# Attention in a hybrid encoder block on 8 cores: the meta keys' V products as two 64-row matmuls, added to opened banks

## The reference

```python
s_grid = einsum('bqhd,bkqjhd->bhqkj', q_r, k_r) * scale + bias       # 8 x 16 neighbours
s_meta = einsum('bqhd,bmhd->bhqm', q_r, km) * scale + mbias          # 16 meta keys
p = softmax(concatenate([s_meta, s_grid], axis=-1), axis=-1).astype(v.dtype)
out = einsum('bhqm,bmhd->bqhd', p_m, vm) + einsum('bhqkj,bkqjhd->bqhd', p_g, v_r)
```

## Time and profile before

| | |
|---|---|
| median of 3 runs | 1762.98 us (1759.71 to 1766.43) |
| the profiled execution | 1759.94 us |
| its span, slowest core (core 1) | 1758.4 us (cores 1739.4 to 1758.4) |
| mean granted TensorE clock, core 1 | 0.984 |
| busy: TensorE / VectorE / ScalarE | 1690.5 / 998.7 / 821.0 us |

### The profile page before, as it was taken

The page is one execution under the profiler, slowest core; times in us unless marked ns, Lnnn a source line. Parts: engine busy times, 40 slices in busy tenths (PEclk is TensorE's granted clock), DMA queues, the critical chain, the costliest instruction groups (busy, mean ns, idle before and its releaser), DMA issues.

```text
span 1758.4 us, 39342 instructions; the slowest of 8 cores (1739.4 to 1758.4 us)
## 1 busy us (share of the span) xinstructions
PE 1690.5 (96%) x13896; PEld 874.5 (50%) x13896; DVE 998.7 (57%) x1907; ACT 821.0 (47%) x1219; POOL 124.6 (7%) x202
## 2 busy tenths in 40 slices
PE   8898999999999999999999998999999999999998
PEld 3344544444455555655666654444444444444443
DVE  4344443442466675766777765555665566556654
ACT  4355656331256765677777762332333233323332
POOL 0012021111100000000000020000000000000000
PEclk9899999999999999999999999999999999999999
DMA  9689668673555566566533469634464345524421
GB/s 273 206 237 294 216 208 266 184 193 123 165 155 135 164 168 187 152 182 175 146 122 98 129 211 275 186 105 118 127 173 143 94 124 162 165 83 137 138 96 61
DMA packets 163814, 289.21 MB, mean 164 GB/s; under 512 B 70627, under 2 KB 92643, under 8 KB 155047
## 3 DMA queue, kind: packets, MB, share of 16 engines
q1 hardware_dynamic: 110167, 155.04, 30.6%
q0 software_dynamic: 37184, 95.66, 18.8%
q10 hardware_dynamic: 16272, 35.99, 6.6%
HBM read 194.90 MB, written 100.90 MB: 168 GB/s over the span
## 4 chain that ended last, share of the span: by engine, by line
PE 77%; DMA 6%; issue 5%; ACT 4%; DVE 4%; SPq 2%; ACTq 1%; POOL 0%; DVEq 0%; POOLq 0%
PE bankpair L433 19%; PE bankpair L949 9%; PE bankpair L407 9%; PE bankpair L380 9%; PE bankpair L593 7%; PE bankpair L625 7%; PE bankpair L926 6%; PE bankpair L1061 4%; PE bankpair L1030 3%; ACT sb_PT L1036 2%; DMA sb_Wp<-w_pool 2%; SPq L479 2%; DMA at_s<-sb_ATT 1%; PE bankpair L1049 1%; DVE sb_PT L1042 1%
## 5 line engine op out<-in xcount | busy, mean ns | idle before, releaser
L1036 ACT ACTIVATE sb_PT<-bankpair 128x1024 bf16<-128x1024 f32 (+1 forms) x368 | 318.9, 921 | 152.4 <-PE bankpair L1030 112.1
L433 PE MATMUL bankpair<-sb_Wo,sb_MIX 128*128 128x512 bf16 x1536 | 337.0, 381 | 3.0 <-DVE sb_MIX L417 3.0
L433 PEld LDWEIGHTS bankpair<-sb_Wo,sb_MIX 128*128 128x128 bf16 x1536 | 151.0, 98 | 187.1 <-issue 8.6
L1042 DVE TENSOR_TENSOR sb_PT<-sb_PT,sb_FT 128x1024 bf16<-128x1024 bf16 (+1 forms) x264 | 174.7, 667 | 107.5 <-ACT sb_PT L1036 104.8
L949 PE MATMUL bankpair<-sb_Wz,sb_HT 128*128 128x512 bf16 x768 | 195.2, 382 | 3.1 <-ACT sb_PM L979 2.7
L926 PE MATMUL bankpair<-sb_HT,sb_Wq 128*128 128x512 bf16 x768 | 196.1, 384 | 2.1 <-DVE sb_QT L217 2.0
L593 PE MATMUL bankpair<-sb_HT,sb_Wk 128*128 128x512 bf16 (+1 forms) x832 | 192.2, 386 | 4.8 <-DVE sb_HT L580 3.7
L625 PE MATMUL bankpair<-sb_Wv,sb_HT 128*128 128x512 bf16 x816 | 186.7, 383 | 2.7 <-DVE sb_Wv L217 2.7
L380 PE MATMUL bankpair<-sb_HT,sb_Wg 128*128 128x512 bf16 x768 | 181.5, 379 | 0.0
L441 ACT ACTIVATE sb_junk<-sb_Y 128x1024 bf16<-128x1024 f32 x48 | 50.7, 1057 | 266.5 <-DVE sb_Y L436 266.5
L407 PE MATMUL bankpair<-sb_HT,sb_Wg 128*128 128x512 bf16 x768 | 167.7, 379 | 0.0
(11 more groups left out here) (104 smaller groups left out, 1758.4 us busy)
## 6 DMA issues: line engine op xcount, KB each, us to landing
sb_X<-xall SPq DMA_DIRECT2D x51, 512.0 KB, 6.4
sb_XR<-xall SPq DMA_DIRECT2D x48, 512.0 KB, 3.8
y<-sb_O POOLq DMA_DIRECT2D x48, 512.0 KB, 2.9
sb_HT<-hT_s SPq DMA_DIRECT2D x23, 1024.0 KB, 7.7
sb_KR<-kT_s SPq DMA_DIRECT2D x14, 1024.0 KB, 7.1
sb_UW<-u_s SPq DMA_DIRECT2D x54, 256.0 KB, 9.5
kT_s<-sb_KTs POOLq DMA_DIRECT2D x13, 1024.0 KB, 9.3
v_s<-sb_Vs POOLq DMA_DIRECT2D x49, 260.0 KB, 3.9
```

The source lines that it names most:

```text
L433: S.op('tensor', lambda e, po=po, kc=kc, cg=cg, j=j: e.matmul(banks[po][:, :], MIX[:, kc, j * 128:(j + 1) * 128], Wo[kc // 4][:, kc % 4, c ...
L1036: S.op('scalar', lambda e: e.activation(out=PT[ps][0:nk, bi, :, 0:n].rearrange('p (a b) q -> p a b q', a=2), in_=bank2[sp][0:nk, :].rearra ...
L1042: S.op('vector', lambda e: e.tensor_tensor(out=PT[ps][0:nk, bi, :, 0:n], in0=PT[ps][0:nk, bi, :, 0:n], in1=bl['E'](hs), op=ALU.mult), read ...
```

## The change

The meta keys' V product of a unit becomes two matmuls of 64 rows: `half` 0 and 1 take heads 0 to 3 and 4 to 7 of the group, so that a bank belongs to a half and not to a `par`, and VMb is [128, 2, 264]. A function `pv_plan` says for each unit in which step of the next one it is issued and whether it opens its banks:

- successor of 3 or 4 steps that starts with a pair: V products open both banks, meta is added ahead of the QK of step 2 and norm 0 follows there;
- successor of 3 steps that starts in the middle of a pair: meta comes behind the QK of step 1, adds to bank 4 and opens bank 5;
- successor of 2 steps: meta opens both banks behind the QK of the pair.

Combos use 128 rows everywhere, VC's rows 64 to 127 being cleared where a tile has one chunk. The stores of ATT all go by SyncE.

```diff
                 def v_combo(tl, w):
+                    if len(tl['ch']) == 1:
+
+                        S.op('vector', lambda e: e.memset(VC[w][64:128, :], 0.0), writes=[('VC', w, 1)])
                     for hh, i in enumerate(tl['ch']):
...
-                def p2_pvmeta(ui, par):
+                def p2_pvmeta(ui, opens, ends=False):
                     t, s, G = units[ui]
-                    n = TILES[t]['nq'] * 16
-                    S.op('tensor', lambda e: e.matmul(
-                        banks[4 + par][:, 0:260], PM[t % 2][:, G, s, :], VMb[:, G, par, :, :].rearrange('p a b -> p (a b)'),
-                        start=True, stop=False), reads=[('PM', t % 2, G)] + VMR, writes=[PS(4 + par)])
+                    for half in range(2):
+                        rows = slice(64 * half, 64 * half + 64)
+                        S.op('tensor', lambda e, half=half, rows=rows: e.matmul(
+                            banks[4 + half][:, 0:260], PM[t % 2][rows, G, s, :], VMb[rows, G, 0:260],
+                            start=(opens or (half == 1 and not ends)), stop=(ends and (half == 0 or nblk[ui] <= 2))), reads=[('PM', t % 2, G)] + VMR, writes=[PS(4 + half)])
...
+                    for q in range(4):
+                        jj, par = 2 * half + q // 2, q % 2
                         h = 2 * (4 * G + jj) + par
...
-                        late.append(lambda: S.op('gpsimd' if 9 <= t < 13 else 'sync', lambda e: e.dma_start(
+                        late.append(lambda: S.op('sync', lambda e: e.dma_start(
...
+                nblk = [len(unit_blocks(u)) for u in units]
+                first_step = [sum(nblk[:i]) for i in range(len(units))]
+
+                def pv_plan(ui):
+
+                    nb = nblk[ui]
+                    nn = nblk[ui + 1] if ui + 1 < len(units) else 2
+                    even = ui + 1 == len(units) or first_step[ui + 1] % 2 == 0
+                    opens = even and nn == 2
+                    lead = [lambda bi=bi: p2_pv(ui, 0, bi, bi == 0 and not opens, False) for bi in range(nb - 1)]
+                    tail = lambda last: [lambda: p2_pv(ui, 0, nb - 1, False, last)]
+                    half1 = [lambda bi=bi: p2_pv(ui, 1, bi, bi == 0 and even and not opens, bi == nb - 1 and (nb > 2 or not even or opens)) for bi in range(nb)]
+                    n0, n1 = [lambda: p2_norm(ui, 0)], [lambda: p2_norm(ui, 1)]
+                    if nn == 2:
+                        return 0 if even else 1, opens, {0: lead, 1: tail(True) + n0 + half1 + n1}
+                    if even:
+                        return 2, False, {0: lead, 1: tail(False) + half1[:2], 2: half1[2:] + n1}
+                    return 1, False, {0: lead, 1: tail(True) + n0 + half1[:2], 2: half1[2:] + n1}
...
                     for ui, b in steps[k:k + 2]:
                         if b == 0:
                             unit_begin(ui)
+                        if b == 2 and ui > 0 and pv_plan(ui - 1)[0] == 2:
+                            p2_pvmeta(ui - 1, False, True)
+                            p2_norm(ui - 1, 0)
+                    for ui, b in steps[k:k + 2]:
                         p2_qk(ui, b)
                     for ui, b in steps[k:k + 2]:
+                        if b < 2 and ui > 0 and pv_plan(ui - 1)[0] == b:
+                            p2_pvmeta(ui - 1, pv_plan(ui - 1)[1])
+                    for ui, b in steps[k:k + 2]:
                         unit_step(ui, b)
-                for part in pv_steps(len(units) - 1):
+                p2_pvmeta(len(units) - 1, True)
+                for part in pv_plan(len(units) - 1)[2].values():
```

More of the change, by code:

```diff
@@ L894, in build_program @@
                         S.op('sync', lambda e, jj=jj, par=par, p0=p0: e.dma_start(
-                            out=VMb[p0:p0 + 16, :, par, jj, :],
+                            out=VMb[p0:p0 + 16, :, (2 * (jj % 2) + par) * 65:(2 * (jj % 2) + par) * 65 + 65],
                             in_=v_d[VM + 16:VM + 32, :].rearrange('m (g q f) -> m g q f', g=2, q=8)[:, :, 2 * jj + par, :]),
@@ L1007, in unit_blocks @@
                         b = dict(nk=nk, parts=[(i, 7 * w, 1, 64 * k) for k, i in enumerate(tl['ch'])], V=VC[w],
-                                 vres=[('VC', w, k) for k in range(len(tl['ch']))])
+                                 vres=[('VC', w, k) for k in range(2)])
                         if tl['xs'] is None:
@@ L1054, in p2_pv @@
+                def p2_pv(ui, half, bi, opens, last):
                     t, s, G = units[ui]
-                    n = TILES[t]['nq'] * 16
                     ps = ui % 2
                     bl = unit_blocks(units[ui])[bi]
-                    nk = bl['nk']
-                    for jj in range(4):
+                    for q in range(4):
+                        jj, par = 2 * half + q // 2, q % 2
                         h = 2 * (4 * G + jj) + par
-                        S.op('tensor', lambda e, jj=jj, h=h: e.matmul(
-                            banks[4 + par][:, jj * 65:(jj + 1) * 65], PT[ps][0:nk, bi, par * 4 + jj, :],
-                            bl['V'][0:nk, h * 65:(h + 1) * 65], start=False, stop=(last and jj == 3)),
-                             reads=bl['vres'] + [('PT', ps, bi)], writes=[PS(4 + par)])
@@ L1066, in p2_norm @@
-                def p2_norm(ui, par):
+                        S.op('tensor', lambda e, q=q, jj=jj, par=par, h=h: e.matmul(
+                            banks[4 + half][:, q * 65:(q + 1) * 65], PT[ps][:, bi, par * 4 + jj, :],
+                            bl['V'][:, h * 65:(h + 1) * 65], start=(opens and q == 0), stop=(last and q == 3)),
+                             reads=bl['vres'] + [('PT', ps, bi)], writes=[PS(4 + half)])
+                def p2_norm(ui, half):
                     t, s, G = units[ui]
@@ L1076, in p2_norm @@
                     S.op('vector', lambda e: e.tensor_tensor(
-                        out=ATT[at][0:n, :].rearrange('p (a b c) -> p a b c', a=8, b=2)[:, 4 * G:4 * G + 4, par, :], in0=accv()[:, :, 0:64],
+                        out=ATT[at][0:n, c0:c0 + 256].rearrange('p (a c) -> p a c', a=4), in0=accv()[:, :, 0:64],
                         in1=rec[0:n, rs].unsqueeze(2).to_broadcast([n, 4, 64]), op=ALU.mult),
-                         reads=[PS(ab), ('rec', par)], writes=[('ATT', at)])
-                    if G == 1 and par == 1:
+                         reads=[PS(ab), ('rec', half)], writes=[('ATT', at)])
@@ L1081, in p2_norm @@
+                    if G == 1 and half == 1:
                         t0 = tl['t0']
[L1082 removed]
+                        late.append(lambda: S.op('sync', lambda e: e.dma_start(
                             out=at_d[t0:t0 + n * 4, :].rearrange('(r c) f -> r c f', c=64)[:, 16 * s:16 * s + 16, :], in_=ATT[at][0:n, :]),
                              reads=[('ATT', at)], writes=[('at_d', t, s)], dma=('sA', at)))
[L1086 to L1098 removed]
@@ L1131, in unit_step @@
                             late.pop(0)()
-                    for f in pv_steps(ui - 1)[b] if ui > 0 and b < 3 else []:
+                    for f in pv_plan(ui - 1)[2].get(b, []) if ui > 0 else []:
                         f()
-                    if nb == 2 and b == 1 and ui > 0:
-                        for f in pv_steps(ui - 1)[2]:
-                            f()
                     if b == nb - 1:
```

23 lines of the change are left out of this document (5 added, 18 removed).

## The result

The changed kernel takes 1.0103 times as long as the one before, with an interval of 1.0072 to 1.0134: about 18 us more. The profiled execution took 1777.31 us; its slowest core (core 3) has a span of 1775.8 us, where core 1 of the kernel before had 1758.4. (The ratio leaves out executions in which the cores of a die had a lower granted clock, which both kernels have.)

The account below looks back on a forecast made before the run. TensorE, busy 96% of the span, was taken to bound the kernel. Terms -12.2 + 2.9 + 9.8 + 16.4 + 1.3 = +18.2 us, less 1.5 given back, made +16.7: 1779 us as a median, range 1762 to 1788.

Parts of the forecast that it names:

- The short units: Units followed by one of tiles 0 or 4: meta waits for VectorE's bank 5 norm; +14.9 us net, +16.4 gross.
- The clock, nothing: Attention: TensorE stands about 1 us at a time, granted clock still 0.99, so nothing charged for the clock.
- The odd starts: 24 units whose successor starts mid-pair: meta opening bank 5 waits for VectorE's norm; +7.2 us net, +9.8 gross.
- The free places: Meta pairs in 111 units: two 64-row matmuls run side by side, saving 0.11 us each, -12.2 us gross.
- rival 4: Meta pairs: the two matmuls do not overlap, 111 x 0.11 us more, +29 us, 1791; chance 0.07.
- The switch: 24 units where meta (64x128) precedes combo blocks (64x64): the shape switch costs 0.12 us each, +2.9 us.
- Clears at the start: Start of the attention stretch: VectorE's VMb clear shrinks, a clear of VC is added; +0.6 us.
- Given back later: QK's waits for ScalarE in the attention: TensorE's later arrival shortens the next of them; 1.5 us taken off.
- The stores, nothing: 16 ATT stores moved from GpSimd's to SyncE's queue: no cost; 10 us at most if loads came late.
- Rival 1: Meta's banks are free when it comes, so the waits do not bind: -9.6 us, 1753; chance 0.08.
- Rivals 2 and 3: 2: only short units wait, +8.4 us, 1771, chance 0.15. 3: half those waits also absorbed, 0 to +3, 1765, 0.12.
- The sign that I named: Changed profile: 64-row meta matmuls wait for VectorE's norms, some 25 us in all against 8.3 before.

Follow-up runs that it names:

- the version without the waits: Changed kernel with short places and odd starts both undone, every meta product added at a pair's head to banks V products opened (but the last two units): ratio 0.9988.

## Why the prediction was right

The forecast of the measured time was +16.7 us, by standing TensorE at both kinds of places, and it came out as about +18 in the ratio, +16.3 in the attention (16.1 of the 16.7 were forecast there). The mechanism was right in both kinds of places. But the terms were less right than their sum; by the table of tiles:

- **The short units, 14.9 net:** 16.8 was measured, 6.0 in tile 0 (forecast 5.3) and 10.8 in tile 4 (forecast 9.6). The pair of tile 0 took 6.07 us, where the same pair took 5.25 before and 0.84 were to be added, so the reading by place was good there. It was good in tile 4 too: core 7, whose clock stayed at 1.00 in both kernels, went from 25.65 to 35.57 us, 9.9 more. In the mean of the cores it is 0.9 more, which goes with the clock.
- **The clock, nothing:** this step failed, by about 1 us. The forecast took the 0.99 of the earlier trace rows, a mean over 604 us, to say that standing times of 1 us cost nothing. In tile 0 that held; at the start of tile 4 the clock fell to 0.50 on seven of eight cores, which cost them 1.2 to 2.4 us against core 7.
- **The odd starts, 7.2 net:** first places 0.43 us of standing forecast, 0.41 measured; tile ends +0.23 forecast, 0.44 − 0.23 = +0.21 measured. Right in both sizes.
- **The free places, −12.2 gross:** two metas take 0.12 us against a forecast of 0.11, and 0.08 a unit are lost when they share rows. Overlap was right, and rival 4 falls with it.
- **The switch, 0.12 each:** 0.09 measured, 0.7 us less in all. With the measured sizes (eight times 0.11 gained, 0.41, 0.21 + 0.11 and two times 0.09 lost) tiles 9 to 11 should have grown by 0.03 each, with those of the forecast by 0.13; they grew by 0.06 in the mean. The drain at a change of mode that the Trainium skill names (TensorEngine Tiling, Key Properties) was there, and small.
- **Clears at the start, +0.6:** not shown. The part ahead of the attention grew by 0.7, but in the other versions that keep the clears it takes 451.1 to 461.3 us.
- **Given back later, −1.5:** QK's waits for ScalarE went down by 0.8 us only. Tiles 1 to 3 and 5 to 11 together became 2.0 us shorter where the forecast left them at +1.3. About 1 us of that is the scatter of the clock, by an estimate from the traces behind the table: over the eight cores it fell 14 times in tiles 3, 7 and 8 before and 10 times after, and such a tile takes 1.8 to 3.6 us longer than on the cores without a fall. What the rest is I can't say.
- **The stores, nothing:** this step failed. The forecast asked only what the stores do to SyncE's queue. It did not ask what they had held back on GpSimd's. Tile 12 and 13 together cost 1.5 us in the changed kernel, 2.4 when the stores alone are moved, and tile 12 alone 4 us or more in the versions that gained elsewhere. It is one reason why the version without the waits, which should have been a clear gain, was none; with the stores back on GpSimd its 5.0 us are still within the scatter of the times.

So that the sum was met within half a microsecond is luck: +1.9 (short units, 0.9 of it clock), +1.2 (stores, 1.5 less what the forecast gave these two tiles) and −3.3 (long tiles) cancel. **Rival 1** (waits do not bind) is out by the short places' 16.8 us; its own number, −9.6 us, is somewhat beyond what the versions without the waits give in the attention (−5.0 with the stores on GpSimd, −7.8 and −7.0 with the loads held back). **Rivals 2 and 3** are out by tiles 9 to 11 and by the odd starts' timeline: norm 1 is late by 0.4 us, no less than was read. The sign that I named, some 25 us of waits at the meta products, came out as 21.8, in which an odd start counts 0.14 of its 0.41.

What stays open: why TensorE has one gap of 2.0 to 2.8 us at its QK while the loads run. It leaves tile 12 with the loads, which is shown (with the loads held back some cores have one in tile 13); what the sequencer waits for is not. On core 1 of the changed kernel the DMA engines are busy by nine tenths in most slices from 992 to 998 us, and one packet of the instruction queue is among what they move, so a late fetch of instructions is a guess that fits, and no more. Open too is why the clock falls at tile 4 and not in tile 0.

## What to carry to other kernels

A matmul that opens a bank inherits the wait for the bank's last reader, one that adds to it does not: before putting a cheap product first, read when the reader of the unit before ends, and if that is later than TensorE's arrival, let a product that comes late anyway open the bank and add the cheap one at the next point where its shape is in use. When an operation is moved off a queue, ask not only what it delays on the new one but what it held back on the old one. A granted clock of 0.99 over 600 us says nothing of a single tile, so read the clock tile by tile and core by core before a difference of 1 us is explained otherwise. And a forecast that is met as a sum can be wrong in three terms, so compare by stage.

## What the runs showed of the hardware

- Two matmuls of 260 columns on rows 0 to 63 and 64 to 127, into different banks, take 0.12 us together; on the same rows a unit takes 0.08 us more (the second may then run beside QK's matmuls).
- From the end of VectorE's last read of a bank to the start of the TensorE matmul that opens it: 0.14 us in tile 0, as the 0.15 of the earlier trace rows.
- A 0.17 us reciprocal between two multiplies of 0.42 costs only 0.08 us; a second multiply costs 0.52. The durations of single instructions of VectorE do not add up to distances.
- Loads issued early by one engine slow those of another: on core 1 the first two of tile 12's six 256 KB loads of the normalised input landed 13.2 and 13.5 us after their issue with the gate weights' loads beside them, 6.1 and 6.4 without.
- TensorE's granted clock fell from 1.00 to 0.50 at the start of tile 4, at two standing times of 0.87 and 1.17 us, on seven of eight cores (the eighth has the same two), and behind the one gap of 2.0 to 2.8 us in tile 12 on five; six pairs of tile 0 with 0.6 to 1.2 us of standing left it at 1.00. A tile with such a stretch of some 3 us takes 1 to 4 us longer than on the cores without.
